# Whole gate and whole up matrices as the unit of transfer in a streamed mixture of experts

## What is computed

```
scores = sigmoid(x @ w_router)             # 256 tokens, 64 experts
eidx   = the 8 best experts of a token, out of the 4 best groups of 8
y      = sum over the 8: weight * ((silu(x @ w_gate[e]) * (x @ w_up[e])) @ w_down[e])
out    = y + swiglu(x, shared gate, shared up, shared down)
```

## Time and profile before

| what | value |
|---|---|
| median of three runs | 2792.86 us |
| the profiled execution's own time | 2791.81 us |
| its span, first to last instruction | 2790.1 us |
| around the span | 1.7 us |
| granted TensorE clock, mean | 0.988 |
| PE busy | 2640.1 us, 95% |
| packets of SP's queue (q1) | 266544, 715.19 MB |
| MoE layer 0, stretch 244.3 to 857 us | 612.7 us |
| MoE layer 1, stretch 1038 to 1618 us | 580.0 us |

### The profile page before, as it was taken

How to read it: one execution, slowest core, us unless ns; L and a number is a source line. 1 busy time by engine, 2 the same in 40 slices (tenths; PEclk the granted TensorE clock), 3 DMA queues, 4 the chain that set the end, 5 groups by cost and what they waited for, 6 DMA issues and landing times.

```text
span 2790.1 us, 42685 instructions
## 1 busy us (share of the span) xinstructions
PE 2640.1 (95%) x16682; PEld 1840.6 (66%) x16682; DVE 1550.6 (56%) x2621; ACT 1003.7 (36%) x1378; POOL 264.4 (9%) x304
## 2 busy tenths in 40 slices
PE   7999998899899989999998999999999999999998
PEld 5986444344347774444443478898788888988887
DVE  5865434334325663333233366688766666778665
ACT  4523222222125542222222243356433433564433
POOL 1401121221210002121212100000000000000000
PEclk9999999999999999999999999999999999999999
DMA  9934999999998528999999965554455555545553
GB/s 371 273 137 182 369 380 382 398 355 384 399 405 288 207 73 308 353 385 354 357 361 395 381 223 191 185 166 151 166 197 194 189 194 183 166 148 198 175 181 105
DMA packets 309708, 733.31 MB, mean 263 GB/s; under 512 B 50156, under 2 KB 191604, under 8 KB 283672
## 3 DMA queue, kind: packets, MB, share of 16 engines
q1 hardware_dynamic: 266544, 715.19, 70.1%
q0 software_dynamic: 34560, 8.25, 1.7%
q10 hardware_dynamic: 8424, 7.39, 0.9%
HBM read 962.35 MB, written 1.05 MB: 345 GB/s over the span
## 4 chain that ended last, share of the span: by engine, by line
PE 82%; DMA 8%; DVE 3%; issue 3%; ACT 3%; SPq 1%; DVEq 0%; ACTq 0%
PE G L1717 16%; DMA wide<-in_moe_w_up_dram 7%; PE Y L1409 6%; PE Y L1410 5%; PE Y L1411 5%; PE U L1740 4%; PE B L1740 3%; PE B L1433 3%; PE U L1433 3%; PE G L1433 3%; PE M L1433 3%; PE U L1409 2%; PE G L1409 2%; PE U L1410 2%; PE U L1411 2%
## 5 line engine op out<-in xcount | busy, mean ns | idle before, releaser
L2157 DVE TENSOR_TENSOR part_lo<-ring,part_hi 128x2048 fp32r<-128x2048 f32 x240 | 548.6, 2290 | 285.3 <-ACT part_hi L1031 285.0
L1031 ACT ACTIVATE part_hi<-ring 128x2048 fp32r<-128x2048 f32 x240 | 459.1, 1914 | 485.4 <-PE Y L1411 255.8
L1717 PE MATMUL G<-wide,gathered 128*32 128x512 f32 (+1 forms) x2144 | 466.8, 600 | 48.8 <-issue 48.5
L1717 PE MATMUL G<-arena,gathered 128*32 128x512 f32 (+1 forms) x1696 | 466.7, 600 | 23.0 <-DMA wide<-in_moe_w_up_dram 20.2
L1717 PEld LDWEIGHTS G<-wide,gathered 128*32 128x32 f32 (+1 forms) x2144 | 133.4, 115 | 218.7 <-issue 218.6
L1409 PE MATMUL Y<-part_hi,rows_hi 128*128 128x512 f32 x608 | 239.9, 395 | 4.9 <-DVE rows_lo L2461 3.0
L1410 PE MATMUL Y<-part_lo,rows_hi 128*128 128x512 f32 x608 | 237.8, 391 | 0.0
L1411 PE MATMUL Y<-part_hi,rows_lo 128*128 128x512 f32 x608 | 237.5, 391 | 0.0
L1135 ACT ACTIVATE swi<-G 128x256 f32<-128x256 f32 x72 | 27.6, 384 | 571.5 <-PE G L1717 571.5
L2412 DVE SCALAR_TENSOR_TENSOR swi<-G,slot_gate,swi 128x256 f32<-128x256 f32 x72 | 34.8, 483 | 345.2 <-ACT swi L1135 329.2
L1717 PEld LDWEIGHTS G<-arena,gathered 128*32 128x32 f32 (+1 forms) x1696 | 123.2, 116 | 154.1 <-issue 151.5
(11 more groups left out here) (598 smaller groups left out, 5853.3 us busy)
## 6 DMA issues: line engine op xcount, KB each, us to landing
wide<-in_moe_w_down_dram SPq DMA_DIRECT2D x128, 1024.0 KB
ring<-in_ffn_w_up_dram SPq DMA_DIRECT2D x88, 1024.0 KB, 5.3
arena<-in_moe_w_gate_dram SPq DMA_DIRECT2D x128, 512.0 KB
arena<-in_moe_w_up_dram SPq DMA_DIRECT2D x128, 512.0 KB
wide<-in_moe_w_gate_dram SPq DMA_DIRECT2D x128, 512.0 KB
wide<-in_moe_w_up_dram SPq DMA_DIRECT2D x128, 512.0 KB
ring<-in_ffn_w_down_dram SPq DMA_DIRECT2D x44, 1024.0 KB, 4.9
ring<-in_w_in_dram SPq DMA_DIRECT2D x40, 1024.0 KB, 5.2
```

The source lines that it names most:

```text
L1031: eng.activation(part_hi[:, n % SPLIT, :], ring[:, slot, :], ACT.Copy).then_inc(hi_ready, 1)
L1717: last = mm(bank["G"][first:first + width], lhsT=gathered[p // 2 % 2][:, k, at:at + width], rhs=units[tile][:, :, k % (K // 2), :], start= ...
L2157: eng.tensor_tensor(part_lo[:, n % SPLIT, :], ring[:, slot, :], part_hi[:, n % SPLIT, :].bitcast(F32), ALU.subtract).then_inc(lo_ready, 1)
```

## The change

The two granules that held half of gate and half of up become one granule with all of gate (part 0) and one with all of up (part 1), each in one transfer of 1 MB. PE makes 16 steps per unit in place of 8: eight for gate with 256 moving columns into the first half of bank G, then eight for up into the second half. The stationary operand is loaded for each of the 16. `pair_half` now tells that the gate products are done, `pair_up` that the up products are. In unit 0 the small table products stand after steps 4, 8, 12 and 16.

```diff
-LANDS = [32 if part < 2 else 16 for _, part, _ in GRANULES]
+LANDS = [16 for _ in GRANULES]
...
                     if part < 2:
-                        ks, halves = slice(K // 2 * part, K // 2 * (part + 1)), to.rearrange("p (a k n) -> p a k n", a=2, k=K // 2)
-                        for c, w in enumerate((A["moe_w_gate"], A["moe_w_up"])):
-                            eng.dma_start(halves[:, c], chosen(w, e, "(p k)")[:, ks, :]).then_inc(landing, 16)
+                        eng.dma_start(view_a(to), chosen((A["moe_w_gate"], A["moe_w_up"])[part], e, "(p k)")).then_inc(landing, 16)
...
-                def landed_wide(p, tile, half):
+                def landed_wide(p, tile, part):
...
-                        return over_wide[i].rearrange("p a (k n) -> p a k n", k=K)[:, :, K // 2 * half:K // 2 * (half + 1), :]
-                    return landed(n, half).rearrange("p (a k n) -> p a k n", a=2, k=K // 2)
+                        return view_a(over_wide[i][:, part, :])
+                    return view_a(landed(n, part))
...
-                def up(p, ks):
-                    if ks[0] == 0:
+                def up(p, steps):
+                    if steps[0] == 0:
...
-                    for k in ks:
-                        if k % (K // 2) == 0:
-                            units[:] = [landed_wide(p, tile, k // (K // 2)) for tile in range(len(MOE[p]))]
+                    for step in steps:
+                        part, k = step // K, step % K
+                        if k == 0:
+                            units[:] = [landed_wide(p, tile, part) for tile in range(len(MOE[p]))]
...
-                            last = mm(bank["G"][first:first + width], lhsT=gathered[p // 2 % 2][:, k, at:at + width],
-                                      rhs=units[tile][:, :, k % (K // 2), :], start=(k == 0), stop=(k == K - 1),
-                                      skip_group_check=True)
-                        if k == K // 2 - 1:
-                            last.then_inc(pair_half, 1)
-                    if ks[-1] == K - 1:
-                        last.then_inc(pair_up, 1)
+                            last = mm(bank["G"][first:first + width, part, :], lhsT=gathered[p // 2 % 2][:, k, at:at + width],
+                                      rhs=units[tile][:, k, :], start=(k == 0), stop=(k == K - 1), skip_group_check=True)
+                        if k == K - 1:
+                            last.then_inc((pair_half, pair_up)[part], 1)
...
-                        up(p, (0, 1))
+                        up(p, range(0, 4))
                         blocks_before()
-                        up(p, (2, 3))
+                        up(p, range(4, 8))
                         turn_gates()
-                        up(p, (4, 5))
+                        up(p, range(8, 12))
                         over_tables()
-                        up(p, (6, 7))
+                        up(p, range(12, 16))
                         slot_tables(0)
                     else:
-                        up(p, range(K))
+                        up(p, range(2 * K))
```

## The result

The kernel after the change takes 2763.62 us (median of 4 runs, 2762.33 to 2768.86) against 2792.99 us for the kernel before in the same comparison. The ratio is 0.989, 95% interval 0.9871 to 0.9909: 29 us faster, with 25 to 36 in the interval. Repeated later it was 0.9906 (0.989 to 0.9922). The forecast of 2779 us had the sign, and the wide range of 2761 to 2799 held the time, but the gain is 29 us and not the 13 of its sum. The profiled execution took 2762.33 us, its span 2760.6.

The account below looks back on a forecast made before the run. PE and DMA were taken as both close to their limits in the two MoE layers, meeting at part 1's landing. From 2791.8 us, -5 - 10 - 3 + 3 + 2 = -13 gave 2779 us, own range 2770 to 2787, 8-in-10 range 2761 to 2799.

Parts of the forecast that it names:

- What bounds the kernel: Two MoE layers: PE and DMA both near their limits, meeting where PE waits for part 1; better transfers bring at most 60 us.
- Packets, queue full: Gate and up transfers at a full queue: 8 KB packets in place of two of 4 KB, -5 us, bounds -12 and +6.
- Packets, slow stretches: Dips in DMA rate while gate or up rows are read: -10 us taken, bounds 0 and -29.
- Issues: SP's queue: each gate or up granule issued once, not twice; -3 us, 10 us at most, 0 at least.
- PE and the instruction fetches: PE's doubled matmuls in mixed units, +3 us, and DMA time for some 32 more instruction fetches, +2 us.
- +3 for mixed units: Gate/up products in 56 mixed units: 128 matmuls of 256 columns for 64 of 512, +0.05 us each, bounds 0 and +15.
- rival of a slow feed: Mixed units: 128 matmuls take 7.7 us, 0.9 more, so +25 us and 2804 us in all; chance 0.03.
- rival of a slower kernel by fetches: Weight transfers: extra instruction fetches delay landings, up to 37 us; up to 2814 us, 2805 at three quarters; chance 0.10.
- rival of PE that cannot be fed: Mixed units: instructions cannot reach PE fast enough for 128 matmuls in about 6.9 us; 2804 us or more; chance 0.03.
- T units, silu, unit 0, the ring: T units' weight loads hidden under matmuls, ACT's waits, first unit's gathered rows, freeing of places: nothing for each.
- faster rival: Gate and up transfers: slow stretches go entirely and the issue gain is full, -39 us, 2757 us; chance 0.08.

Follow-up runs that it names:

- k_halves: Kernel after, with each gate or up matrix in two transfers of 512 KB, rows k 0 to 3 then 4 to 7, 4 KB packets: 2782.93 us, ratio 0.9958.
- swapped_rows: Kernel after, one transfer per gate or up matrix, its row halves swapped in SBUF so packets are 4 KB: 2781.69 us, ratio 0.9951.
- far_halves: Kernel after, gate and up matrices in two 512 KB transfers; where two places come free together, both first halves precede both second halves: 2789.21 us, ratio 0.9989.
- narrow_products: Kernel before with its old transfers, but each gate/up product of 512 columns made as two of 256: 2795.38 us, ratio 1.000.
- parity_halves: Kernel after, each gate or up matrix in two transfers, even partitions then odd ones, packets of 8 KB: 2779.51 us, ratio 0.9933.
- p_halves: Kernel after, each gate or up matrix in two transfers, partitions 0 to 63 then 64 to 127, packets of 8 KB: 3484.05 us, ratio 1.2418.

## Why the prediction was right and wrong

*What bounds the kernel* was read rightly: two resources close together, the landings meeting PE in the middle of a unit. PE's busy time stayed, the first such wait in the chain is 0.84 us where it was 1.84, and the waits in total came to 47.8 us where about 50 were forecast. The waits from which that forecast came were 69.3 us and not 66, as a row had been left out.

*Packets, queue full* is the step that failed: -5 us, with bounds of -12 and +6, where k_halves and swapped_rows show 16 and the full windows 16 as well. So the mechanism was right, but this term of the sum had less than a third of its size, and 16 lies outside its bounds. The bounds took one window of 7 us and one of 6.3 for the same rate and 409 GB/s from a single down window of 4.8 us for the other. A window of that length holds a part of a dip or an edge, and their scatter of 11 GB/s was as large as the difference sought, 10. Windows of four matrices without a dip, or the median of thousands of packets, would have given 2.5 to 3% at once: the trace of before already had 8 KB packets beside 4 KB ones, 309 against twice 159 ns.

*Packets, slow stretches* was set at -10 of 29 us, and the part of the gain that k_halves and swapped_rows keep is 13. The third was a choice between 0 and 29 that no row supported, so that its size came out near is luck. The place was right, the reason was not quite: swapped_rows has pieces of 4 KB that follow each other at once, and its slow stretches are as short as those of the change. What costs, by the ratio of far_halves, is to come back for the second piece after other matrices; the profiled executions bear that out only in part. Some 18 of 37 us of slow stretches went with the change; the rest remains, so something that whole matrices meet too is in them.

*Issues*, -3: k_halves issues twice what swapped_rows does, at 0.0007 of a difference, 2 us with an interval of 6 around it. Not seen.

*PE and the instruction fetches*, +5 together: narrow_products has both and came out at 0, within 3.4 us. The step's +3 for mixed units is 2 us by the chain, 7.04 for 7.00. (The prediction's rival of a slow feed counted 0.9 us more for 7.7 us a unit; against 7.00 that is 0.7, and +20 us in place of +25.) The fetches in layer 1 rose from 32 to 46 and cost nothing that shows, so the rival of a slower kernel by fetches fell. The rival of PE that cannot be fed fell too: 128 matmuls in 7.04 us are 55 ns each, the pace of the burst, kept up in the mixed units of the chain that have no wait. The Trainium skill's 62 ns per matmul with hardware decode off ("TensorE: Matmul & The Clock Gate", section "Wait — 56ns, not 53.3ns?") is not what binds here.

*T units, silu, unit 0, the ring*, 0 each: the T unit's gate and up steps take 6.91 us (6.87 before), and no new wait stands among those of PE. As forecast.

The sum then reads -16 - 13 + 0 = -29 us, with 2 us of PE inside it, in place of -5 - 10 - 3 + 3 + 2 = -13. The time lies outside the 2770 to 2787 us that the forecast had as its own, and inside 2761 to 2799 only because that range took in a part of the faster rival. This rival, 2757 us, was the nearer one, 7 us off against 15, though not for its reason: it had the slow stretches go entirely and the packets still at 5.

**What stays open.** How much of the 13 us is the late second visit, since times and profiles differ on it, and why it costs; what the remaining slow stretches are; why the two layers show 20 to 23 of the 28.5 us only; and the 10 us of parity_halves. The 3 us between far_halves and the kernel before lie within the interval.

## What to carry to other kernels

Where a streamed weight bounds a stage, cut transfers so that a partition's row in memory goes as one packet, and read all of a matrix before the next; 2.5 to 3% of these matrices' transfer time hung here on packets of 8 KB over 4 KB, and by the ratios nearly as much on not coming back for the second half. Cutting a transfer in two by rows cost no more than its smaller packets where the second half followed at once; cutting it into partitions 0 to 63 and 64 to 127 took the rate from 387 to 238 GB/s. When a rate is to be compared at 2%, use the median of many packets or windows of several whole transfers at the same place of the program, not single windows of 5 us.

## What the runs showed of the hardware

A packet of 8 KB took 309 ns and one of 4 KB 159 ns at a full queue, with medians within 3 ns of these in every kernel but p_halves. Where gate and up went in transfers of partitions 0 to 63 and 64 to 127, and down in whole ones, 238 GB/s moved at a share of 0.99; two transfers of every second partition did not slow down in this way. Returning to the other half of 8 KB rows after another matrix cost 9 us by the ratios (0.9989 for 0.9958) over the pairs of places that come free together, with the same packets and the same bytes; the profiled layers show 2.7 us of it. And 128 matmuls with 128 weight loads could be fed in 7.04 us, unit after unit.
